# A three-product gemm with one 512-column matmul in place of two of 256 columns, for twelve tiles of cross attention keys and queries

## What is computed

```python
q = (h @ wq).reshape(b, n, X_HEADS, X_HEAD_DIM)
kv = (m @ wkv).reshape(b, nm, 2, X_HEADS, X_HEAD_DIM)
k, v = kv[:, :, 0], kv[:, :, 1]
s = jnp.einsum("bqhd,bkhd->bhqk", q, k).astype(jnp.float32) * (X_HEAD_DIM ** -0.5)
p = jax.nn.softmax(s, axis=-1).astype(v.dtype)
o = jnp.einsum("bhqk,bkhd->bqhd", p, v).reshape(b, n, X_HEADS * X_HEAD_DIM)
return o @ wo
```

## Times and profile before

| | |
|---|---|
| median of 3 runs | 893.02 us |
| time of the profiled execution | 893.71 us |
| its span, first to last instruction | 891.9 us |
| TensorE busy, weight loads busy | 880.6 us (99%), 754.1 us (85%) |
| VectorE busy | 647.9 us (73%) |
| ScalarE busy | 493.8 us (55%) |
| mean granted clock of TensorE | 0.998 of full speed |
| chain that ended last: TensorE's share | 92% |

### The profile page before, as it was taken

One profiled execution on the slowest core, in us unless ns is written; L12 is line 12 of the kernel. 1 busy time (PEld: TensorE's weight loads), 2 busy tenths in 40 slices (PEclk: granted clock), 3 DMA queues, 4 the chain that ended last, 5 costly groups with the idle time before them and its releaser, 6 DMA issues.

```text
span 891.9 us, 13262 instructions
## 1 busy us (share of the span) xinstructions
PE 880.6 (99%) x5100; PEld 754.1 (85%) x5100; DVE 647.9 (73%) x1024; ACT 493.8 (55%) x880; POOL 92.8 (10%) x123
## 2 busy tenths in 40 slices
PE   8999999999999999999999999999999999999997
PEld 6988997889889888888789887898888888888886
DVE  5789975574879688789856846677687774766774
ACT  5855665474477465566635366676555772324341
POOL 1324100010010000000133300011031100000000
PEclk9999999999999999999999999999999999999999
DMA  9745423453654455556418644344266554564531
GB/s 314 248 155 177 163 97 131 153 193 115 189 200 154 142 175 185 208 181 245 166 60 283 211 143 142 107 161 170 95 229 195 169 186 142 189 212 165 189 142 48
DMA packets 99502, 152.25 MB, mean 171 GB/s; under 512 B 2608, under 2 KB 66352, under 8 KB 99184
## 3 DMA queue, kind: packets, MB, share of 16 engines
q1 hardware_dynamic: 99040, 150.68, 50.3%
q10 hardware_dynamic: 288, 0.47, 0.2%
q0 software_dynamic: 112, 0.26, 0.1%
HBM read 150.35 MB, written 1.05 MB: 170 GB/s over the span
## 4 chain that ended last, share of the span: by engine, by line
PE 92%; DVE 5%; ACT 2%; issue 1%; DMA 1%; POOL 0%; DVEq 0%; POOLq 0%; SPq 0%; ACTq 0%
PE ps L578 28%; PE ps L571 19%; PE ps L1080 13%; PE ps L636 8%; PE ps L1084 7%; PE ps L668 4%; PE ps L743 2%; PE ps L754 1%; PE ps L831 1%; DVE sb_wlo L2266 1%; PE ps L707 1%; PE ps L1028 1%; PE ps L932 1%; PE ps L1224 1%; ACT sb_whi L1631 1%
## 5 line engine op out<-in xcount | busy, mean ns | idle before, releaser
L2266 DVE TENSOR_TENSOR sb_wlo<-sb_ring,sb_whi 128x1024 fp32r<-128x1024 f32 (+2 forms) x169 | 203.5, 1215 | 81.6 <-ACT sb_whi L1631 81.1
L1631 ACT ACTIVATE sb_whi<-sb_ring 128x1024 fp32r<-128x1024 f32 (+2 forms) x169 | 174.0, 1046 | 101.5 <-PE ps L636 69.5
L578 PE MATMUL ps<-sb_whi,sb_tb 128*128 128x512 f32 (+2 forms) x520 | 128.8, 387 | 0.0
L578 PEld LDWEIGHTS ps<-sb_whi,sb_tb 128*128 128x128 f32 x520 | 93.9, 188 | 17.3 <-issue 1.0
L578 PE MATMUL ps<-sb_whi,sb_ta 128*128 128x512 f32 (+1 forms) x240 | 57.8, 380 | 0.0
L636 PE MATMUL ps<-sb_wlo,sb_tb 128*128 128x512 f32 (+2 forms) x224 | 57.7, 380 | 0.0
L1519 POOL TENSOR_SCALAR sb_st<-sb_st 128x1 f32<-128x1 f32 x14 | 7.3, 524 | 451.6 <-ACT sb_probs L1895 451.6
L2224 ACT ACTIVATE sb_b<-sb_b 128x512 f32<-128x512 f32 x9 | 5.7, 632 | 79.7 <-DVE sb_b L2695 79.7
L578 PEld LDWEIGHTS ps<-sb_whi,sb_ta 128*128 128x128 f32 x240 | 42.3, 188 | 8.6 <-issue 0.5
L636 PEld LDWEIGHTS ps<-sb_wlo,sb_tb 128*128 128x128 f32 x224 | 41.3, 188 | 7.6
L2695 DVE TENSOR_REDUCE sb_b<-ps 128x256 f32<-128x512 f32 x36 | 23.8, 685 | 28.6 <-PE ps L1084 28.6
(11 more groups left out here) (430 smaller groups left out, 2068.0 us busy)
## 6 DMA issues: line engine op xcount, KB each, us to landing
sb_ring<-in_w_in SPq DMA_DIRECT2D x32, 1024.0 KB, 5.4
sb_ring<-in_w_up SPq DMA_DIRECT2D x18, 1024.0 KB, 5.1
sb_ring<-in_w_down SPq DMA_DIRECT2D x11, 1024.0 KB, 7.4
sb_ring<-in_w_ffn_down SPq DMA_DIRECT2D x11, 1024.0 KB, 7.5
sb_ring<-in_w_ffn_gate SPq DMA_DIRECT2D x9, 1024.0 KB, 5.3
sb_ring<-in_w_ffn_up SPq DMA_DIRECT2D x9, 1024.0 KB, 5.4
sb_ring<-in_w_xkv SPq DMA_DIRECT2D x8, 1024.0 KB, 5.6
sb_ring<-in_w_out SPq DMA_DIRECT2D x4, 1024.0 KB, 5.1
```

The lines of the kernel that those rows point to most:

```text
L578: pe.matmul(o, l, r, start=(start and n == 0), stop=False, skip_group_check=True)
L1631: act.activation(piece_pair(m)[0], src, ACT.Copy).then_inc(s("hi_done"), 1)
L2266: dve.tensor_tensor(low, pieces[m][1], high.bitcast(F32), ALU.subtract).then_inc(s("lo_done"), 1)
```

## The change

Twelve pieces go from `cols_half` to a new function `cols_wide`: the four of `xkv1` (keys of heads 2 and 3), the four of `w_xq0` and the four of `w_xq1` (all queries). The other users of `cols_half` stay. A tile now has a bank to itself: 8 matmuls of 512 columns, then 8 of 256 into the bank's first half, 16 in place of 24. To read a tile, ScalarE copies the bank's second half to its place in SBUF (`take_low`), and VectorE then adds the first half to it (`add_high`), which releases the bank. So for two tiles ScalarE has two instructions of 128 x 256 in place of one of 128 x 512, and VectorE has two new ones of 128 x 256. `scoresx` now waits for VectorE's release of both tiles.

```diff
+            def cols_wide(name, half, js=(0, 1)):
+                for j in js:
+                    m, w = next_piece(name, hi_done)
+                    key = f"{name}.{half}.{j}"
+                    banks.take(pe, key, next_g())
+                    o = bank[banks.at[key][0]]
+                    for i in range(KT):
+                        tile_there(i)
+                        pe.matmul(o[:, :], w[0][:, i, :], TB[:, i].rearrange("p two n -> p (two n)"),
+                                  start=i == 0, stop=False)
+                    pe.wait_ge(*lo_done(m))
+                    for i in range(KT):
+                        mm = pe.matmul(o[:, 0:S], w[1][:, i, :], TB[:, i, 0, :], start=False, stop=i == KT - 1)
+                    mm.then_inc(banks.fill(key), 1)
+                    piece_used(m, mm, key)
...
             def scoresx(h, o, r, n):
                 if r == 0:
-                    pe.wait_ge(*banks.empty(f"w_xq{h // 2}.{h % 2}"))
+                    for j in range(2):
+                        pe.wait_ge(*banks.empty(f"w_xq{h // 2}.{h % 2}.{j}"))
...
             attend("attx", X_HEADS, readyx, by_rows(scoresx, (S, S)), valuesx, (S, S),
-                   {(0, "scored"): [(cols_half, "w_xq1", hTx, 0, (0,))], (1, "scored"): [(cols_half, "w_xq1", hTx, 0, (1,))],
-                    (1, "turned"): [(cols_half, "w_xq1", hTx, 1, (0,))], (2, "turned"): [(cols_half, "w_xq1", hTx, 1, (1,))],
+                   {(0, "scored"): [(cols_wide, "w_xq1", 0, (0,))], (1, "scored"): [(cols_wide, "w_xq1", 0, (1,))],
+                    (1, "turned"): [(cols_wide, "w_xq1", 1, (0,))], (2, "turned"): [(cols_wide, "w_xq1", 1, (1,))],
...
+            def take_low(key, dst, scale=1.0):
+                for j in range(2):
+                    act.wait_ge(*banks.full(f"{key}.{j}"))
+                    act.activation(dst[:, j * S:(j + 1) * S], bank[banks.at[f"{key}.{j}"][0]][:, S:2 * S], ACT.Copy,
+                                   scale=scale).then_inc(s("wide_low"), 1)
...
+            def add_high(key, dst, scale=1.0):
+                for j in range(2):
+                    wide[0] += 1
+                    dve.wait_ge(s("wide_low"), wide[0])
+                    t = dst[:, j * S:(j + 1) * S]
+                    dve.scalar_tensor_tensor(t, bank[banks.at[f"{key}.{j}"][0]][:, 0:S], scale, t, ALU.mult, ALU.add
+                                             ).then_inc(banks.release(f"{key}.{j}"), 1)
...
+                if p in (1, 2):
+                    add_high(f"xkv1.{p - 1}", xkT_flat[:, 512 * (p + 1):512 * (p + 2)])
                 ahead(first1 + 2 * p + 4)
...
-            ahead_of("w_xq0", 6)
+            ahead_of("w_xq0", 5)
+            add_xq(0)
+            ahead_of("w_xq0", 7)
+            add_xq(1)
...
-            attend("attx", X_HEADS, (S, S), take_x, {}, pieces_of["f1.in0"][0] + 1)
+            attend("attx", X_HEADS, (S, S), take_x, {1: [(add_xq, 2)], 2: [(add_xq, 3)]}, pieces_of["f1.in0"][0] + 1)
```

More of the change, by code:

```diff
@@ L988, in _ @@
             for j in range(2):
-                cols_half("xkv1", memT, 0, (j,))
+                cols_wide("xkv1", 0, (j,))
             scores1(1)
             turn_probs1(0)
-            cols_half("xkv1", memT, 1, (0,))
+            cols_wide("xkv1", 1, (0,))
             values1(0)
-            cols_half("xkv1", memT, 1, (1,))
+            cols_wide("xkv1", 1, (1,))
             for p in (2, 3):
@@ L1015, in _ @@
             for half in range(2):
-                cols_half("w_xq0", hTx, half)
+                cols_wide("w_xq0", half)
             def readyx():
@@ L1020, in readyx @@
                     for half in range(2):
-                        pe.wait_ge(*banks.empty(f"xkv{c}.{half}"))
+                        for key in ((f"xkv0.{half}",), [f"xkv1.{half}.{j}" for j in range(2)])[c]:
+                            pe.wait_ge(*banks.empty(key))
                         pe.wait_ge(*banks.empty(f"xkv{2 + c}.{half}"))
@@ L1865, in _ @@
                 if p in (1, 2):
-                    take_rows(f"xkv1.{p - 1}", xkT_flat[:, 512 * (p + 1):512 * (p + 2)])
+                    take_low(f"xkv1.{p - 1}", xkT_flat[:, 512 * (p + 1):512 * (p + 2)])
                 ahead(first1 + 2 * p + 4)
@@ L1982, in take_xq @@
             def take_xq(h):
-                take_rows(f"w_xq{h // 2}.{h % 2}", B[2][:, h * 512:(h + 1) * 512], scale=X_DIM ** -0.5)
+                take_low(f"w_xq{h // 2}.{h % 2}", B[2][:, h * 512:(h + 1) * 512], scale=X_DIM ** -0.5)
             for h in range(2):
@@ L2575, in take_att1, with add_xq @@
                 split_out(*(t[:, p, :] for t in mixT), psum(key, S)).then_inc(banks.release(key), 1)
+            wide = [0]
+            def add_high(key, dst, scale=1.0):
[5 more added lines that the diff above has]
+                                             ).then_inc(banks.release(f"{key}.{j}"), 1)
+            def add_xq(h):
+                add_high(f"w_xq{h // 2}.{h % 2}", B[2][:, h * 512:(h + 1) * 512], X_DIM ** -0.5)
             first1 = pieces_of["xkv1"][0]
```

## The result

The changed kernel takes 895.84 us (median of 19 runs, 893.95 to 897.42) against 893.20 (19 runs, 892.39 to 893.81, among them the three with the median of 893.02). The ratio is 1.0031, with a 95% interval of 1.0025 to 1.0037: slower by 2.6 us, more than the 0.2% that can be told from nothing.

The account below looks back on a forecast made before the run. The prediction took TensorE, busy 880.6 of 891.9 us, as the bound, with any new wait paid in full. A 2.4 us stall less 1.0 saved gave +1.4, a median of about 894.5 us, range 893.3 to 896.6.

Parts of the forecast that it names:

- The wide pieces: Twelve pieces on TensorE: 0.09 us saved on each of eleven, 0.02 on the first of `w_xq0`, 1.0 us in all.
- The additions: VectorE's new additions from PSUM: 0.42 us each, about 0.8 us for a pair.
- ScalarE's pair: ScalarE's two copies of 128 x 256 in place of one of 128 x 512: about 0.2 us more per pair.
- The margins at heads 1 and 2: Queries ready before TensorE reaches the scores, by 1.1 us at head 1 and 0.7 at head 2: no wait.
- The shifted banks: Banks given out in turn shift by two from the self attention on; claimed to cost nothing.
- The wait at head 3: Head 3's scores wait for additions queued on VectorE behind two passes over head 0's output: TensorE loses 2.4 us.
- The sum with the clock up: Whole kernel, stall less saving with TensorE's clock staying up: +1.4 us, median about 894.5 us, chance 0.50.
- rival B: The stall at head 3 also takes TensorE's clock down: 1.6 us on top, +3.0 in all, 896.0 us; chance 0.34.
- Its C: No stall at head 3's scores, the change only saves 1.0 us: 892.0 us; chance 0.07.
- Its D: A second stall, at the scores of head 2: TensorE waits 0.5 us more, 895.0 us; chance 0.05.

Follow-up runs that it names:

- add_first: The changed kernel with VectorE's two additions for head 3 moved ahead of its read of head 0's output; 891.74 us, ratio 0.9992 to the kernel before.
- add_last: The changed kernel with VectorE's two additions for head 3 one step later, behind the low part that follows them; 897.23 us.
- stall_only: The kernel before, with head 3's scores also waiting until VectorE has read head 0's output, no wide products; 894.34 us, ratio 1.0020.
- keep_busy: The changed kernel with eight more matmuls of 512 columns, result unused, just ahead of head 3's scores; 894.57 us, ratio 1.0021 to the kernel before.
- all_keys: add_first with the four pieces of `xkv0` wide too, sixteen in all; 891.80 us, ratio 0.9992 to the kernel before.
- stall_longer: The kernel before, with head 3's scores also waiting for the low part behind VectorE's read of head 0's output; 897.12 us, ratio 1.0045.
- last_pair_narrow: The changed kernel with the last two pieces (queries of head 3) in the old form, read by ScalarE alone; 892.26 us, ratio 0.9997 to the kernel before.

## Why the prediction was right, and where it was off

**The wide pieces (predicted 1.0 us saved; 0.87 measured).** The three pieces of `w_xq0` that stand behind one another gained 0.08 to 0.10 each, the first one 0.02 (3.80 to 3.78), as said. What was mis-sized is the 0.09 for the others: the keys gained 0.05 to 0.09 and the pieces of `w_xq1` 0.06 or 0.07 (213.06 to 216.02 before, 211.73 to 214.62 after). I had taken the distance from a stretch where one wide piece follows another, and these stand behind other work. The term as a whole is 0.13 us too large, small beside the wait.

**The additions (predicted 0.42 us each, some 0.8 a pair; 0.415 and 0.74 to 0.76 measured).** Right, the nearest row was the one of the same types. ScalarE's pair takes 0.64 to 0.66 us, 0.05 to 0.07 more than the one copy and not the 0.2 of the prediction, which had added two durations that overlap. The margins at heads 1 and 2, predicted as 1.1 and 0.7 us, came out as 1.3 and 0.9 (additions over at 205.56 and 213.68, scores at 206.85 and 214.62): no wait there. The shifted banks brought no new wait either.

**The wait at head 3 (predicted 2.4 us; 2.42 measured).** Right in place, releaser, and size: the wait itself is 2.26 us, the start 2.42 us later than before. It is VectorE's order that makes it (add_first, add_last), not VectorE's load.

**The sum with the clock up (predicted +1.4; the six lower runs are about +1.65 above the kernel before's lower ones, 894.13 to 892.48).** 0.13 of the difference is the pieces. Another 0.08 stands in the profiles of stall_only and keep_busy, where the scores right behind a wait take 1.97 us in place of 1.89.

**The clock (rival B, predicted +1.6 on top, 896.0 us, chance 0.34).** Mechanism and price were right: about 1.7 us, with the median at 895.84. What was off is the chance. I gave the case in which the clock stays up 0.50 and named its 894.5 as the predicted time; in fact thirteen runs of 19 lie in the upper group, so B was the likelier one, and the predicted time is 1.3 us too low. The range of 893.3 to 896.6 held because it was drawn around both cases; that the median fell into it says nothing for the choice between them. I argued from the start of the trace, where the clock fell after 1.35 us of idling, and set against it that TensorE is full on both sides of the new gap. stall_only shows what that argument was worth: after 1.6 us idle, full on both sides, no run of 11 has the extra 1.7 us; after 2.3 us most runs do. The one row near the start, with its half-empty surroundings, could not tell how this gap compares. It could not even tell how often a fall follows the gap that it shows, as the last section has it.

**Rivals C and D of the prediction** did not happen. Its C (which is not the theory C of the experiments) was that there is no wait at all; that came only when VectorE's order was changed, in add_first and all_keys, or when head 3's queries stayed in the old form. Its D was a second wait, at the scores of head 2; no profile has one.

## What to carry to other kernels

When a read is split between two engines, the second half inherits the second engine's queue: look for what that half is queued behind, and above all whether one of those instructions waits for the very engine that will wait for it. Here moving two instructions ahead of a read that could not start yet was worth 3.4 to 4.1 us, some four times what the wide products bring. And price a new gap on TensorE twice, once for its length and once for the clock behind it: here a gap of 2.3 us cost 2.4 and, in most runs, 1.7 more.

## What the runs showed of the hardware

How often the extra loss came, told by the group that a run lies in, by the idle stretch of TensorE before the scores of head 3, with full work on both sides: 0.41 us in none of 11 runs (keep_busy), 1.6 us in none of 11 (stall_only), 2.26 us in 13 of 19 (the changed kernel), 2.7 us in three or four of 5 (stall_longer; one of them is at 896.09, between the groups), 3.4 us in 4 of 5 (add_last). So the same program on the same data falls into two groups of runs, and a median over few of them can land in either. In all eight falls of the eleven profiled executions, five near the start and three at head 3, the granted clock was 0.50 for 3.4 us. The page "TensorE: Matmul & The Clock Gate" of the Trainium skill, section "HAM oscillation — how this bites in real kernels", has idle gaps bring the clock back to 1.2 GHz; the runs agree, and show it for single gaps in an otherwise full stream.

The kernel before has a smaller spread of the same kind (892.2 to 892.6 and 892.8 to 893.9), and its profiled execution has a fall near 14 us. The profiles tell what it is. All eleven kernels have the same instructions there and the same idle stretch of 1.34 or 1.35 us before them, yet five of the profiled executions have a fall (the kernel before, the changed kernel, add_first, keep_busy, last_pair_narrow) and six have none. Here is stall_only, without one, against the two groups of the earlier trace rows:

```profile
12.03 3.00 PE L578 MATMUL ps<-sb_ta,sb_whi 128*128 128x256 f32 x16 [1.35 <-DVE sb_ta L2290]
14.87 1.12 PE L743 MATMUL ps<-sb_ta,sb_wlo 128*128 128x256 f32 x8
```

From the first group of products on line 578 (12.03) to the third the six take 6.67 to 6.69 us and the five 7.34 to 7.99, and each of the five is in the upper part of its kernel's runs. So whether the clock falls after this gap differs from one execution to the next, with nothing changed in this stretch of the program, and the fall costs 0.7 to 1.3 us, which is the size of the spread. No experiment acted on this fall itself. Nor was it tested whether the two falls hang together: none of the changed kernel's six lower runs is between 894.8 and 895.4, where a fall at the start alone would put it.

One product of 512 columns cost 230 ns and two of 256 cost 239, each with its own weight load. The saving of 9 ns for a pair is over three times the 2.5 ns that would follow from the section "Back-to-back issue gap" of the same page of the Trainium skill, whose formula is for the isolated gap and has no weight load in it.
